# Two transformer blocks on one core: the arena of on-chip pieces starts 32 bytes later

## The reference

```
def first_block(x, mem, ...):
    for l in range(DEPTH):                       # DEPTH = 2
        h = x @ w_in[l]                          # 1024 x 7328
        c_q, c_kv, k_pe, dq, dk, dv, mq, gate_pre = jnp.split(h, splits, axis=-1)
        ...                                      # three attention branches
        merged = (g[:, :, 0] * (o_mla @ wb[:MLA_OUT]) + g[:, :, 1] * (o_diff @ ...)
                  + g[:, :, 2] * (o_mem @ ...))
        x = _layernorm(DEEPNORM_ALPHA * x + merged @ w_out[l], ln1_g[l], ln1_b[l])
        f = jnp.square(jax.nn.relu(x @ mlp_w1[l])) @ mlp_w2[l]
        x = _layernorm(DEEPNORM_ALPHA * x + f, ln2_g[l], ln2_b[l])
    return x

def second_block(x, p, ...):
    for l in range(DEPTH):
        u = _rmsnorm(h, norm_mix_g[l])
        (s_z, s_xbc, s_dt, g_q, g_f, g_i, g_g, m_q, m_k, m_v, m_i, m_f, m_o,
         gates) = _split(u @ w_in[l], IN_SIZES_2)
        ...                                      # three scan branches, gated and merged
        h = h + merged @ w_out[l]
        up = _dwconv(_rmsnorm(h, norm_ffn_g[l]) @ w_up[l], ffn_conv_w[l], ffn_conv_b[l])
        h = h + (jax.nn.silu(a_half) * v_half) @ w_down[l]
        h = h + (p[l] @ w_ple[l]) * jax.nn.sigmoid(h @ w_ple_gate[l])
    return _rmsnorm(h, final_norm_g)
```

## Time and profile before

| | |
|---|---|
| median of three runs | 2476.62 us (2476.34 to 2481.26) |
| the profiled execution's own time | 2482.01 us |
| its span, first to last instruction | 2480.2 us |
| PE busy in the span | 2432.6 us, 98% |
| DVE, ACT, POOL busy | 1774.4, 1463.5, 286.9 us |
| granted TensorE clock, mean | 0.995 |

### The profile page before, as it was taken

The page is one execution under the profiler, slowest core; times in us unless marked ns, Lnnn a source line. Parts: engine busy times, 40 slices in busy tenths (PEclk is TensorE's granted clock), DMA queues, the critical chain, the costliest instruction groups (busy, mean ns, idle before and its releaser), DMA issues.

```text
span 2480.2 us, 43108 instructions
## 1 busy us (share of the span) xinstructions
PE 2432.6 (98%) x17744; PEld 2226.1 (90%) x17744; DVE 1774.4 (72%) x2827; ACT 1463.5 (59%) x2176; POOL 286.9 (12%) x224
## 2 busy tenths in 40 slices
PE   8999999999999999999999999999999999999998
PEld 7888999988889899799999799998799999899996
DVE  4558675565576755668768887885598768887875
ACT  5547555445466555477655655664678656656654
POOL 0000002000000000101223720000012207500000
PEclk9999999999999999999999999999999999999999
DMA  7554476555544565564566646656555557645663
GB/s 247 160 139 124 157 250 193 187 184 170 139 127 145 180 194 187 169 175 138 146 198 186 194 137 192 192 192 195 143 160 145 167 178 205 182 148 189 190 210 127
DMA packets 358919, 430.49 MB, mean 174 GB/s; under 512 B 20616, under 2 KB 286310, under 8 KB 358468
## 3 DMA queue, kind: packets, MB, share of 16 engines
q1 hardware_dynamic: 341312, 401.72, 53.1%
q10 hardware_dynamic: 14340, 14.93, 2.6%
q0 software_dynamic: 3072, 11.10, 1.5%
HBM read 424.44 MB, written 3.24 MB: 172 GB/s over the span
## 4 chain that ended last, share of the span: by engine, by line
PE 88%; DVE 8%; ACT 2%; issue 1%; DMA 1%; POOL 0%; POOLq 0%; ACTq 0%; DVEq 0%
PE ps L112 86%; PE ps L115 2%; DVE wlo L121 2%; DVE hgQ L121 1%; DVE hgA L148 1%; ACT lnv L118 0%; DMA kT<-in_diff_lambda 0%; ACT L118 0%; DVE hgkf L121 0%; DVE hgT L121 0%; DVE hgkb L121 0%; ACT whi L118 0%; DVE sbc L130 0%; DVE kT L121 0%; DVE sz L130 0%
## 5 line engine op out<-in xcount | busy, mean ns | idle before, releaser
L121 DVE TENSOR_TENSOR wlo<-wring,whi 128x1024 fp32r<-128x1024 f32 x766 | 920.4, 1221 | 263.9 <-ACT whi L118 263.1
L118 ACT ACTIVATE whi<-wring 128x1024 fp32r<-128x1024 f32 (+1 forms) x768 | 803.6, 1054 | 415.8 <-PE ps L112 403.0
L112 PE MATMUL ps<-uT,whi 128*128 128x256 f32 x4640 | 815.5, 280 | 4.5 <-DVE wlo L121 4.5
L112 PEld LDWEIGHTS ps<-uT,whi 128*128 128x128 f32 x4640 | 703.7, 188 | 14.2 <-DVE wlo L121 7.4
L112 PE MATMUL ps<-uT,wlo 128*128 128x256 f32 x2320 | 644.5, 278 | 0.0
L112 PEld LDWEIGHTS ps<-uT,wlo 128*128 128x128 f32 x2320 | 435.1, 188 | 0.0
L112 PE MATMUL ps<-xT,whi 128*128 128x256 f32 x2112 | 379.2, 283 | 2.3 <-DVE xT L121 1.1
L112 PEld LDWEIGHTS ps<-xT,whi 128*128 128x128 f32 x2112 | 321.8, 187 | 9.4 <-issue 5.2
L112 PE MATMUL ps<-xT,wlo 128*128 128x256 f32 x1056 | 295.3, 280 | 0.0
L112 PE MATMUL ps<-whi,hid 128*128 128x512 f32 x864 | 270.6, 392 | 0.0
L112 PEld LDWEIGHTS ps<-xT,wlo 128*128 128x128 f32 x1056 | 198.4, 188 | 0.3
(11 more groups left out here) (394 smaller groups left out, 3568.3 us busy)
## 6 DMA issues: line engine op xcount, KB each, us to landing
wring<-in_w_in SPq DMA_DIRECT2D x346, 512.0 KB, 4.1
wring<-in_mlp_w SPq DMA_DIRECT2D x128, 512.0 KB, 4.5
wring<-in_w_up SPq DMA_DIRECT2D x88, 512.0 KB, 4.5
wring<-in_w_down SPq DMA_DIRECT2D x44, 512.0 KB, 4.3
wring<-in_w_branch SPq DMA_DIRECT2D x32, 512.0 KB, 3.4
wring<-in_w_out SPq DMA_DIRECT2D x32, 512.0 KB, 4.3
wring<-in_mem_w_kv SPq DMA_DIRECT2D x16, 512.0 KB, 6.7
wring<-in_w_br_hg SPq DMA_DIRECT2D x16, 512.0 KB, 4.8
```

The lines of the kernel that those rows point to most:

```text
L112: return self.e.matmul(*p, **k) if self.e else Nothing()
L118: return self.e.activation(*p, **k) if self.e else Nothing()
L121: return self.e.tensor_tensor(*p, **k) if self.e else Nothing()
```

## The change

The base of the arena is put at the next byte that is 96 mod 256, where it was the next that is 64 mod 128. In the built program that is 82528 in the place of 82496: every piece in the arena is 32 bytes further on, and keeps its offset. `wring`, `whi`, `wlo`, `cst` and the other fixed tensors stay where they are. Every engine's instructions, their order and their waits are the same.

```
--- before.py
+++ after.py
@@ -365,7 +365,7 @@
     K.lbc = sb("lbc", 64)
     K.posi = ctx.enter_context(nc.sbuf_tensor("posi", [2, 128], I32))
     K.posr = ctx.enter_context(nc.sbuf_tensor("posr", [2, 128], F32))
-    base = (nc.sbuf_base + 63) // 128 * 128 + 64
+    base = (nc.sbuf_base + 191) // 256 * 256 + 96
     K.ar = Arena(nc, base, (nc.sbuf_usable_end - base) // 4 // 64 * 64)
 
     K.ident = cst[:, C_ID:C_ID + 128]
```

## The result

The changed kernel takes 2522.06 us (median of three runs, 2520.72 to 2522.28) against 2476.62 before: a ratio of 1.0182, with a 95% interval of 1.0165 to 1.0199. It is 45 us slower. The forecast was 14 us faster, with a range up to 2510; the second rival, in which the upper rung becomes the rule, had priced this at up to 43 us.

The account below looks back on a forecast made before the run. PE's matmul spacing was taken as the bound. Savings of 12 us (256 columns) and 3.5 us (512), less 1.4 us lost on level pieces, gave 14 us off the 2476.6 us median: 2462.5 us, range 2447 to 2510.

Parts of the forecast that it names:

- the second rival: All float32r products: starts off a common 64-byte step make slow spacing the rule; up to 43 us slower, 2482 to 2520, chance 0.26.
- upper rung: Slower steady spacing of float32r matmul starts: 117.6 ns against 113.3 for 256 columns, up to 233 against 226 for 512.
- What bounds the kernel: PE, busy 98% of the span at full clock: only the distance from one matmul to the next can move the time.
- The row-based 31 us of excess: Float32r products above the lowest spacing: 24 us for 256 columns and 7 us for 512, the most that can be gained.
- get in each other's way unless they start at the same position: PE's streamed read and next-block load: level pieces were clean at 389 ns; those at 64 mod 256 were slower.
- The step that failed: All float32r products at the new 32-byte distance: half the 24 us and half the 7 us were expected to go.
- The 24 us that I halved: 256-column products' slow-spacing cost: uT 11.9 us, xT 8.0, yT 1.7, ym and the like 2.4.
- the rung at 192 is drawn: 256-column products, streamed at 64 against loaded at 128: spacing is drawn when a stretch begins, then kept.
- The level pieces: About 900 512-column matmuls (hid of block 2, hT, merged of block 1), level with the weights: expected to lose 1.4 us.
- uT leaves 276: Sign against the prediction: the long clean uT stretch from 1562.8 us no longer has 276 ns records.
- the last rival: 256-column matmuls: a streamed row off a 64-byte step needs 6.7 ns more each; 79 us, 2556 us, chance 0.10.
- DVE, ACT, DMA, transposes at nothing: Other engines' work, the transposes and loads into the arena: the address shift was to cost nothing, bound below 1% on engines.

Follow-up runs that it names:

- both_shifted: Kernel before with the arena at 96 mod 256 and whi, wlo and cst moved 32 bytes to 160, keeping every distance: ratio 1.0001.
- streams_alone: Not the full kernel: PE alone streams zeros through both matmul forms at several operand distances; 113.3 to 120.0 ns at distances 192 and 0 (256 columns).
- arena_128: Kernel before with only the arena base moved to 82560, level with whi and wlo (distance 0): 2525.81 us, ratio 1.0207.
- loaded_back: Kernel after with merged of block 1, hid of both blocks and hT returned to their former distances: 2514.47 us, 1.0153 to the kernel before.
- streamed_112: Kernel before with the weights in one tensor at 144 mod 256 and the arena at 0, making the distance 112: ratio 1.0233, 2532 us.

## Why the prediction was wrong

**What bounds the kernel** was right: PE's spacing, on rungs that a stretch keeps, and no other engine. The row-based 31 us of excess is 26.9 when all starts are counted.

**That position acts through the two operands that PE reads** was right: both_shifted shows that their relative place counts, and streams_alone that PE alone is enough. That they "get in each other's way unless they start at the same position" was right in its first half at most, and wrong in its second. That position acts at all is why the page I cited gave the wrong sum. By the Trainium skill, "SBUF — State Buffer", section "SBUF: two separate sides", PE never waits on anyone, which would have left the time at 2476.6 us; the runs span 2458 to 2533 us on positions alone. No run here tests that sentence between engines. It can't be carried over to PE's own two operands, since streams_alone finds the rungs with no other engine at work.

**The step that failed** is "The nearest are distance 0, which is clean, and distance 64, which is not. I take the middle". Three things were wrong in it. Distance 0 was clean in the rows only for the 512-column form; the rows had no 256-column product at 0, and arena_128 shows that there it is 120.0 ns, among the slowest. The 24 us that I halved were all of the 256-column form. Second, 32 is in no sense between 0 and 64: the table rises and falls without order. Third, I took distance without a sign. Before was -64 (192), after is -32 (224), and +64 and +32 are other places with other rungs. In the terms of the sum, 12 and 3.5 us less and 1.4 more had been forecast; the table of excess has 33.3 and 6.0 more (256 and 512 columns) and 5.5 more on the level pieces.

**That the rung at 192 is drawn** when a stretch begins fits the two values, ten and eight of 18 with PE alone, though whether chance draws it or something ahead of the stretch fixes it wasn't tested. I drew the wrong lesson. I read a place on which half of the stretches are slow as a poor place, though of the fifteen other multiples of 16 bytes only one, 112, was as quick for 256 columns. What a move could lose was larger than what it could gain, and the "at most 31 us" against "43 us" in the bounds said so already.

**The level pieces** were given 1.4 us of loss and cost 5.5, as excess (0.2 to 5.7); loaded_back gave back 7 to 8, with hid of block 1 among them, which had not been level before.

**The rival that came true** had the right place and price, 43 us against 45, for partly the wrong reason. There is no common step of 64 bytes: both_shifted has neither operand on a multiple of 64 and is as fast as before, arena_128 has both on one and is slow. And the 256-column rung isn't 117.6 ns but a new one of 118.3. What I held against it, that E and PT show no step at 32 bytes, concerns float32, whose records didn't move in the kernel after either. It says nothing of float32r. Of the signs I named, "uT leaves 276" came, and hid of block 2 did leave 389. A record above 281, 285, came as well, and I had tied it to the last rival, of 6.7 ns more in each 256-column matmul. That rival is wrong all the same: the spacing rose to 118.3 ns, not by 6.7, and the time is 2522 and not 2556 us.

**DVE, ACT, DMA, transposes at nothing** was right.

What stays open: what makes these distances good or bad, and what decides at distance 192 between 113.3 and 117.8 ns, or, in the kernel before, between 229 and 233.3 with 512 columns. The runs show the pattern, not a mechanism, and no run tried other column counts or types in this way.

## What to carry to other kernels

Where PE is the bound and equal matmuls differ by a few ns from tile to tile, the positions of the streamed and the loaded operand relative to one another are worth a table, measured by a kernel that runs PE alone; it took two kernels of 0.6 ms here, and for 256 columns the whole kernels came within about 1 ns a matmul of it wherever the weights stood on a multiple of 32 bytes. The table must have the place within 32 bytes as a second entry: without it, streamed_112 was expected at 2464 us and took 2532. A stretch's first matmuls count too where stretches are short. Don't interpolate between two positions, nor carry one from a form to another: the best place for 512 columns, level, was among the worst for 256 (weights at 128 mod 256). Before moving a base, ask whether the present place is one of the few good ones, and move both operands together (by 32 bytes it was free here) if one must move.

## What the runs showed of the hardware that was not expected

- The rate of float32r matmuls depends on the addresses of both operands modulo 256: 113.3 to 122.9 ns for 256 columns and 226.7 to 234.3 for 512, at full clock. 122.9 is distance 4. Four bytes past a multiple of 16 were the dearest places of all for 256 columns: distance 196 gave about 122.
- At some distances two rungs exist for the same matmuls: with 256 columns 113.3 or 117.8 ns at 192, 116.6 or 118.7 at 144, and with 512 columns 226.7 or 228.3 at 240. At 192 the rung was settled at the start of a stretch and then kept.
- At distance 112 a stretch begins at about 118 ns and comes down to 113.3 after some ten matmuls.
- The best rungs are 113.3 and 226.7 ns, one ratio to the columns. The Trainium skill, "TensorE: Matmul & The Clock Gate", section "Back-to-back issue gap", gives for a matmul by itself a fixed 2.5 ns over the columns' time, 216 ns for 512. No stretch of float32r here came below 226.7, and none of 256 columns below 113.3.
- Moving both operands by 32 bytes left the whole kernel's time as it was (1.0001), and moving both by 16 bytes turned 113.4 into 120 ns at distance 112 (256 columns) and, with 512 columns, 234.2 into 226.7 at 96 and 226.7 into as much as 233.3 at 0.
